# Masks of the selected branch by repeated-row loads, and early K/V stores from ScalarE's queue, in a hybrid conformer and sparse-attention block

## The reference, cut to what matters

```python
proj = u @ w_in                                  # u = rms_norm(x); one combined projection
# block importance from the compressed branch, top 16 of 32 blocks of 64 keys for each query
importance = jnp.einsum('bgsn,nm->bgsm', jnp.sum(p_cmp, axis=2), overlap)
sel_score = jnp.where(forced & valid, FORCED_SCORE, jnp.where(valid, importance, MASKED_SCORE))
_, sel_idx = lax.top_k(sel_score, n_sel)
...
# selected branch: softmax over the keys of the chosen blocks alone, causal
mask = key_pos <= tc[:, None, None]
p = masked_softmax(s, mask)
o = g[..., 0:1] * o_cmp + g[..., 1:2] * o_slc + g[..., 2:3] * o_win
```

## Time and profile before

| | us |
|---|---|
| the three executions shown | 6959.97, 7552.63 (median), 7947.71 |
| profiled execution, its own time | 6946.9 |
| its span (core 1, the slowest of 8) | 6945.4 |
| spans of all cores | 6864.7 to 6945.4 |
| PE busy | 6811.0 (98%) |
| DVE busy | 2239.3 (32%) |
| ACT busy | 1169.0 (17%) |
| share of the chain that ended last, PE | 94% |

### The profile page before, as it was taken

One profiled execution on the slowest core, in us unless ns is written; L12 is line 12 of the kernel. 1 busy time (PEld: TensorE's weight loads), 2 busy tenths in 40 slices (PEclk: granted clock), 3 DMA queues, 4 the chain that ended last, 5 costly groups with the idle time before them and its releaser, 6 DMA issues.

```text
span 6945.3 us, 98178 instructions; the slowest of 8 cores (6864.7 to 6945.4 us)
## 1 busy us (share of the span) xinstructions
PE 6812.9 (98%) x37468; PEld 3534.2 (51%) x37468; DVE 2238.7 (32%) x4038; ACT 1169.3 (17%) x2168; POOL 452.0 (7%) x727
## 2 busy tenths in 40 slices
PE   7999999989999999999999999999999999999997
PEld 4644454445555544466654444444444444444665
DVE  5418889544444513324430111111111111111134
ACT  4001110234444410013320000000000000000221
POOL 0000000000000000011100000000000000000110
PEclk9999999999999999999999999999999999999999
DMA  9645655778764355678854456775676766644798
GB/s 253 156 91 96 111 104 106 163 124 146 140 131 101 73 127 121 118 204 290 296 116 79 97 117 135 122 120 121 154 168 116 122 124 154 141 78 81 232 322 310
DMA packets 312533, 1017.19 MB, mean 146 GB/s; under 512 B 27360, under 2 KB 113248, under 8 KB 286720
## 3 DMA queue, kind: packets, MB, share of 16 engines
q0 software_dynamic: 160176, 707.98, 51.8%
q1 hardware_dynamic: 149440, 298.72, 13.1%
q10 hardware_dynamic: 2448, 4.13, 0.2%
HBM read 1381.75 MB, written 202.70 MB: 228 GB/s over the span
## 4 chain that ended last, share of the span: by engine, by line
PE 93%; DMA 3%; DVE 1%; issue 1%; SPq 1%; ACT 1%; DVEq 0%; ACTq 0%; POOLq 0%
PE bank L1403 54%; PE bank L352 28%; PE bank L1435 6%; PE bank L1143 2%; PE bank L1118 2%; DMA xr<-xc_t 1%; SPq L131 1%; DMA p_conv<-cstg 1%; PE bank L769 0%; DMA p_q<-sgb 0%; PE bank L1215 0%; DMA wslot<-w_dn_b 0%; DMA out<-yr 0%; DVE yr L1724 0%; DMA p_kv<-sgb 0%
## 5 line engine op out<-in xcount | busy, mean ns | idle before, releaser
L1403 PE MATMUL bank<-merged,wslot 128*128 128x496 bf16 (+2 forms) x11264 | 2119.4, 351 | 1.7 <-DVE merged L1444 1.7
L352 PE MATMUL bank<-uT,wslot 128*128 128x496 bf16 (+1 forms) x8768 | 1900.2, 375 | 0.0
L1403 PE MATMUL bank<-actq,wslot 128*128 128x496 bf16 (+2 forms) x9216 | 1718.2, 349 | 5.4 <-DMA wslot<-w_dn_b 4.1
L1403 PEld LDWEIGHTS bank<-merged,wslot 128*128 128x128 bf16 x11264 | 1102.1, 98 | 1018.3 <-issue 2.7
L352 PEld LDWEIGHTS bank<-uT,wslot 128*128 128x128 bf16 x8768 | 856.7, 98 | 952.5 <-issue 6.3
L1403 PEld LDWEIGHTS bank<-actq,wslot 128*128 128x128 bf16 x9216 | 901.3, 98 | 821.7 <-issue 8.0
L1595 DVE SCALAR_TENSOR_TENSOR rlE<-bank,acc 128x496 f32<-128x496 f32 (+2 forms) x262 | 173.5, 662 | 1489.0 <-PE bank L1403 1488.6
L1601 ACT ACTIVATE actq<-rlE 128x496 bf16<-128x496 f32 (+2 forms) x262 | 159.0, 607 | 2804.1 <-DVE rlE L1595 2804.1
L665 DVE SCALAR_TENSOR_TENSOR yb<-glu,cps,yb 128x992 f32<-128x992 f32 x480 | 600.0, 1250 | 43.2 <-DVE yb L665 1.8
L1121 ACT ACTIVATE emt<-bank 128x512 bf16<-128x512 f32 (+1 forms) x736 | 349.3, 529 | 367.3 <-PE bank L1118 268.0
L1650 DVE TENSOR_TENSOR ost<-bank,part 128x496 f32<-128x496 f32 x128 | 86.3, 674 | 770.3 <-PE bank L1403 770.3
(11 more groups left out here) (180 smaller groups left out, 3075.5 us busy)
## 6 DMA issues: line engine op xcount, KB each, us to landing
wslot<-w_in_t POOLq DMA_DIRECT2D x150, 1024.0 KB, 10.2
wslot<-w_up_t POOLq DMA_DIRECT2D x122, 1024.0 KB, 8.9
wslot<-w_out_b POOLq DMA_DIRECT2D x96, 1024.0 KB, 6.8
wslot<-w_dn_t POOLq DMA_DIRECT2D x96, 1024.0 KB, 11.3
wslot<-w_dn_b POOLq DMA_DIRECT2D x96, 1024.0 KB, 8.6
p_y<-ost SPq DMA_DIRECT2D x96, 496.0 KB, 7.0
w_out_b<-w_out_t POOLq DMA_DIRECT2D x32, 1024.0 KB, 15.7
w_dn_b<-w_dn_t POOLq DMA_DIRECT2D x32, 1024.0 KB, 15.2
```

The source lines that it names most:

```text
L352: fns = [lambda kc=kc, bk=bk: nc.tensor.matmul(bk[:, 0:n], wt[:, kc * 128:(kc + 1) * 128], rhs[:, kc, lo:lo + n], start=(kc == 0), stop=(k ...
L1403: fns = [lambda kc=kc: nc.tensor.matmul(bk[:, 0:n], wt[:, kc * 128:(kc + 1) * 128], rhs[:, kc, lo:lo + n], start=(kc == 0), stop=(kc == KC ...
```

## The change

Masks: on odd cores `expand` no longer multiplies. `selT` (32 rows) is stored to a DRAM scratch `p_sel[s]`, and per four key tiles two loads fetch rows of it, each repeated over 64 partitions, into `msk`. The product with the triangle stands alone in `diagonal`, at the four jobs before sj0. `sel_transpose` is at wj0+5, the loads at wj0+6 and wj0+7, and the loads of the next q, k and v at wj0+12 in place of wj0+8 (on all cores). Two memsets go and `emats` shrinks. K/V: `evac_kv` can store from another queue; the stores of chunks 0 to 4 go from ACT's.

```diff
+    p_sel = dscr("p_sel", [8, 32, 512], BF16)
...
-            def evac_kv(ci):
+            def evac_kv(ci, q=sp):
...
-                    K.dma(sp, p_kv[ci, :, lo:lo + n], sgb[:, i, 0:n], r=[sgbB[i]], w=[kvcB[ci]])
+                    K.dma(q, p_kv[ci, :, lo:lo + n], sgb[:, i, 0:n], r=[sgbB[i]], w=[kvcB[ci]])
...
-                        evac_kv(c)(0, banks[3 * c + k], bankB[3 * c + k], *g)
+                        evac_kv(c, act)(0, banks[3 * c + k], bankB[3 * c + k], *g)
                 for k, g in enumerate(g3[0:2]):
-                    evac_kv(2)(0, sq[:, k, :], sqB[k], *g)
+                    evac_kv(2, act)(0, sq[:, k, :], sqB[k], *g)
...
-                dense(CH_KV + ci, uc, ucB, g3[2:3] if ci == 2 else g3, evac_kv(ci), tick,
+                dense(CH_KV + ci, uc, ucB, g3[2:3] if ci == 2 else g3, evac_kv(ci, act if ci < 5 else sp), tick,
...
-            KE = 128 if h else 32
-            selT = Tile("selT", [KE, 512], BF16, imp.end)
+            selT = Tile("selT", [32, 512], BF16, imp.end)
...
-            emats = Tile("emats", [KE, 2048], BF16, sm.end)
+            emats = Tile("emats", [32, 1024], BF16, sm.end)
...
             if h:
-                K.op(dve, lambda: nc.vector.memset(emats[:], 0.0), w=[ematB])
-                K.op(dve, lambda: nc.vector.memset(selT[:], 0.0), w=[selTB])
-            K.dma(sp, emats[0:32, :], emat[:, :], w=[ematB])
-            if h:
                 K.dma(sp, selvs[:], selv[:, :], w=[selvB])
                 K.dma(sp, selbs[:], selb[:, :], w=[selbB])
             else:
+                K.dma(sp, emats[:], emat[:, 0:1024], w=[ematB])
...
-                K.op(act, lambda: nc.scalar.copy(out=selT[0:32, :], in_=pst[0:32, 0:512]), r=[bb], w=[selTB])
-
-            def expand(s, jt):
-                bk, bb = ring_bank("aux")
-                lo = max(0, jt * 128 - (1024 + (s % 2) * 512))
-                diag = jt * 128 >= 1024 + (s % 2) * 512
-                K.op(pe, lambda: nc.tensor.matmul(bk[:, lo:512], emats[:, jt * 128:(jt + 1) * 128], selT[:, lo:512], start=True, stop=True),
-                     r=[selTB, ematB], w=[bb])
-                K.op(act, lambda: nc.scalar.copy(out=msk[:, jt, lo:512], in_=bk[:, lo:512]), r=[bb], w=[mskB[jt]])
-                if diag:
-                    K.op(dve, lambda: nc.vector.tensor_tensor(out=msk[:, jt, lo:lo + 128], in0=msk[:, jt, lo:lo + 128], in1=tri[:, 0, :],
-                                                              op=ALU.mult), r=[triB], w=[mskB[jt]])
+                K.op(act, lambda: nc.scalar.copy(out=selT[:], in_=pst[0:32, 0:512]), r=[bb], w=[selTB])
+                K.dma(sp, p_sel[s], selT[:], r=[selTB], w=[pselB[s]])
+
+            def expand(s, j0, j1):
+                src = p_sel[s].rearrange("(j k) q -> k j q", k=2)
+                for k in range(2):
+                    K.dma(sp, msk[k * 64:k * 64 + 64, j0:j1, :], src[k, j0:j1, :].unsqueeze(0).to_broadcast([64, j1 - j0, 512]),
+                          r=[pselB[s]], w=mskB[j0:j1])
+
+            def diagonal(s, jt):
+                lo = jt * 128 - (1024 + (s % 2) * 512)
+                K.op(dve, lambda: nc.vector.tensor_tensor(out=msk[:, jt, lo:lo + 128], in0=msk[:, jt, lo:lo + 128], in1=tri[:, 0, :],
+                                                          op=ALU.mult), r=[triB], w=[mskB[jt]])
...
-                    at(wj0 + 11, lambda s=s: sel_transpose(s))
-                    for jt in range(njt):
-                        at(wj0 + 13 + jt, lambda s=s, jt=jt: expand(s, jt))
+                    at(wj0 + 5, lambda s=s: sel_transpose(s))
+                    for i in range(njt // 4):
+                        at(wj0 + 6 + i // 2, lambda s=s, i=i: expand(s, 4 * i, 4 * i + 4))
+                    for jt in range(njt - 4, njt):
+                        at(sj0 + jt - njt, lambda s=s, jt=jt: diagonal(s, jt))
                 if s + 1 < 8:
-                    at(wj0 + 8, lambda s=s: load_q(s + 1))
+                    at(wj0 + 12, lambda s=s: load_q(s + 1))
                 if qg == 1 and g + 1 < 4:
-                    at(wj0 + 8, lambda g=g: load_kv(g + 1, ("vs", "vw", "ks", "kw")))
+                    at(wj0 + 12, lambda g=g: load_kv(g + 1, ("vs", "vw", "ks", "kw")))
```

More of the change, by code:

```diff
@@ L939, in phase_B @@
             sm = Tile("sm", [128, 12], F32, mx.end)
-            emats = Tile("emats", [KE, 2048], BF16, sm.end)
+            emats = Tile("emats", [32, 1024], BF16, sm.end)
             assert emats.end <= eb["lo"]
+            pselB = [Buf() for _ in range(8)]
             goff = gatesT_off - base
```

## The result

The changed kernel takes 7079.11, 7078.73 and 7073.52 us against 6959.97 and 6958.77 us: ratio 1.0169, 95% interval 1.014 to 1.0199, slower by more than its interval and by less than 2%. The direction was right and the time lies in the range, but the loss is about twice the size.

A forecast was written before the change was run, and what follows sets the result against it. The prediction took core 1's TensorE, busy 6811.0 of 6945.4 us (98%), as the bound. It summed 6946.9 - 24 - 13 + 39 + 18 + 44 = 7011 us, 0.9% slower, range 6950 to 7090.

The forecast's parts named there:

- Expansion matmuls, -24: Odd cores' `expand`: removing 112 matmuls from TensorE, with 2.1 us idle ahead of them, gains 24 us.
- Step to the attention, -13: From conv to attention: without the memsets TensorE's 18.04 us pause shrinks, gaining 13 us (at least 8, at most 18).
- Transpose, +39: `sel_transpose` six jobs earlier: TensorE waits for DVE's selm in all eight stages, losing 39 us (35 to 42).
- Clock, +18 and 6: Lower TensorE clock after eight transpose pauses, losing 18 us (0 to 27), and 2 us after each of three mask waits.
- Mask loads, +44: Masks through SP's ring come late in stages 1 to 3: 15, 14, 9 us plus clock, 44 us (0 to 110).
- the 3.5 us left carry 580 more: Stage 1: of 28 us, 24.5 are shared with POOL's ring; the rest carries 580 packets, so 1310 of 2048 arrive.
- 30 a microsecond beside POOL: Rate at which SP's ring moves mask packets while POOL's ring also has work; 165 a microsecond at idle engines.
- 740 packets: Mask packets still missing in stage 1 when needed, of 2048; 25 us beside POOL, 3 to 5 us at idle engines.
- Stores from ScalarE, 0: Phase A, stores of the first chunks from ScalarE's queue: no net effect, -5 to +4 us.
- one about pays for the other: `first_rstd`: TensorE's sums and chunk 3 come some 2.5 us later, but a 2.33 us wait afterwards goes.
- A, masks in time: Rival, chance 0.28: everything as forecast, but the ring keeps up with the mask loads: 6967 us.
- C: Rival, chance 0.12: rings stay full, masks 23 to 40 us late in the first five stages: 7131 us, 2.7% slower.

The follow-up runs named there:

- the early transpose: Kernel before with only the transpose moved from wj0+11 to wj0+5, expansion still on TensorE: 6990.7 and 6996.2 us.
- without the pair wait: Changed kernel, but the two loads of the same key tiles no longer wait for each other: 6966.7 and 6965.4 us.
- without memsets: Kernel before without its two memsets and with the expansion over 32 rows instead of 128: 6950.9 and 6958.4 us.
- late memsets: Kernel before with the memsets and the load of `emats` moved to job 4 of stage 0's window: ratio 0.9991 (0.9979 to 1.0003).
- the kernel with the late transpose: Changed kernel, paired loads not waiting for each other, stores on SyncE, transpose at job 11, mask loads at 12 and 13: 6973.2 and 6989.0 us.
- run 14: Not a run number: "the run 14 us above" means the changed kernel whose paired loads don't wait for each other, 6966.7 and 6965.4 us.
- a kernel that is late for another reason: Kernel before with the matmul groups of ten output chunks' gate done twice on odd cores: 7088.8 and 7091.7 us, ratio 1.02.

## Why the prediction was right or wrong

- **Expansion matmuls, -24: right, as far as shown.** L1215 is gone; nothing was run that takes them away alone. But the kernels with the early transpose and without the pair wait pause alike for it (43.9 and 45.2 us in the mean), and the second takes 22.8 us less from the first window job to the last product (1080.1 against 1102.9). In the sum the 24 narrower matmuls should have been 2.6 us at the price per column that it uses, not 2.3.
- **Step to the attention, -13: right.** The pause fell from 18.04 to 4.58 us, and stage 0's transpose was reached 8.3 us earlier after a phase A that ended 6.9 us later: 15 on core 1. In the table the step is 9.4 us shorter in the changed kernel, 10.5 without memsets and 15.7 without the pair wait. `sm` was next, as foretold (VectorE waits 7.6 us there for the landing of p_q). The run with late memsets adds that most of such a gain can be paid again within the attention.
- **Transpose, +39: right.** 43.6 less 2.3 in the changed kernel, +41.5 by itself.
- **Clock, +18 and 6: about right where it falls.** The dip per pause is as read (2.3 us against 2.5). The transpose alone makes TensorE busy 13.1 us longer in the attention, and in the changed kernel the clock takes some 22 us, masks included, where 24 were forecast. The time of the whole kernel with the transpose alone shows nothing of it.
- **Mask loads, +44: the step that failed.** The changed kernel has 93.7 us of waits for `msk`, and 112 us of its time go when the pair's wait goes. What failed first is that the sum let all loads go out at once; the diff showed both loads of a pair naming `mskB[j0:j1]`, and the prediction did not apply the rule of `K.dma` to it. The other error is "the 3.5 us left carry 580 more": POOL's load was carried over from the stretch of 1582 to 1618 us in the kernel before, as work that lies beside the masks from the first one on. With the pair's wait gone, POOL's ring was empty for the first 8 us and SyncE's moved 1165 packets in them, up to 210 a microsecond and not 165 (that price was taken from packets of 2 KB in the mean; the masks' have 1 KB). "30 a microsecond beside POOL", read from the earlier trace rows, is right: 35 to 39 there, 32 in the kernel with the late transpose. So without the pair's wait the masks came in time, by 1.1 us in stage 1, where 740 packets were to be missing. The two errors have opposite signs, which is why the number came near at all.
- **Stores from ScalarE, 0: right for the time, not for its reason.** Alone the stores change nothing in the time. But "one about pays for the other" is not what the traces show: the first score comes 5 to 6 us later in every kernel that has them (6.9 us on core 1 of the changed one).
- **Rivals.** A, masks in time, gave 6967 us, and the kernel without the pair wait takes 6966.7: its mechanism was right for the ring and wrong for the kernel as written. That the numbers meet is partly luck: A stood 20 us above its kernel before, the run 14 us above the 6952 us of its chip. Of the signs named beforehand, "waits for msk in all eight stages (then C)" came nearest: seven of eight. C's price did not come, because each wait was 3 to 24 us and not 23 to 40.
- **Not foreseen:** the late pause, 14.5 us far from any line of the change. It shows also in a kernel that is late for another reason.

## What to carry to other kernels

When one tile is filled by several DMAs, look at what the dependency tracker thinks they write: two halves that name the same buffer are served one after the other, each with a full landing, and the issuing queue stands for it with all that is behind. Two rings' counts say how they share only in a stretch in which both have work; over 26 us the same trace seemed to say four and a half for one, and over 5 us one for one. And what another ring has to do at that moment is not fixed: it moves with the engine that frees its buffers, so the change can shift it. A variant that gains nothing is worth a look by stretches, since a gain and a price of like size can stand in it one behind the other.

## What the runs showed of the hardware that was not expected

- While both rings had work they moved like counts of packets, 175 of 1 KB beside 164 of 4 KB in 5 us and 194 beside 191, so the ring with the small packets got a fifth of the bytes; with POOL's ring all but empty SyncE's moved 1052 in 5 us.
- With nothing to wait for in between, loads of 1 KB packets were as good as those of 4 KB (6965 to 6967 against 6969 to 6973 us).
- A matmul over 32 rows between matmuls over 128 rows occupies TensorE's queue longer in the trace than one over 128 rows, 0.15 + 0.32 us against 0.06 + 0.22, though it does a quarter of the work. 112 of them made the attention some 10 us longer, of the 21 that this would give.
- Eight pauses of 5 to 8 us made TensorE's busy time over the same instructions 13.1 us longer (1054.39 against 1041.26 us), by the lower clock behind them.
- The same kernel takes 6947 to 6955 us on two of the chips used and 6962 to 6971 us on two others; kernels must be compared on one chip.
